# Two gate tiles per weight tile in a wide job, a longer ring in the prologue, and scores inside a values tile

## The reference, cut to what matters

```python
sh_x, sc_x, gt_x = jnp.split((jax.nn.silu(c) @ w_ada[l] + b_ada[l])[:, None, :], 3, axis=-1)
h_x = rms_norm(x, norm_g[l]) * (1 + sc_x) + sh_x
px = split_cols(h_x @ w_in[l])
...
x = x + gt_x * (jnp.concatenate([oa, ob, oc, od], axis=-1) @ w_out[l])
```

## Time and profile before

| what | us |
|---|---|
| median of 3 runs (lowest, highest) | 2264.65 (2260.85, 2273.97) |
| the profiled execution | 2272.0 |
| its span | 2270.2 |
| TensorE matmul busy | 2202.0 (97%) |
| VectorE busy | 1414.0 (62%) |
| ScalarE busy | 1010.9 (45%) |
| GpSimd busy | 99.5 (4%) |
| mean DMA rate | 180 GB/s |

### The profile page before, as it was taken

How to read it: one execution, slowest core, us unless ns; L and a number is a source line. 1 busy time by engine, 2 the same in 40 slices (tenths; PEclk the granted TensorE clock), 3 DMA queues, 4 the chain that set the end, 5 groups by cost and what they waited for, 6 DMA issues and landing times.

```text
span 2270.2 us, 30077 instructions
## 1 busy us (share of the span) xinstructions
PE 2202.0 (97%) x11346; PEld 1817.2 (80%) x11346; DVE 1414.0 (62%) x2097; ACT 1010.9 (45%) x1494; POOL 99.5 (4%) x106
## 2 busy tenths in 40 slices
PE   5999999999999999999989999999999999999998
PEld 1576888997778888888769888888888888888887
DVE  2248654646845676777776544778777877644455
ACT  3343242334545543555466443544444444444453
POOL 1000100102000121000010000000000000000000
PEclk8999999999999999999999999999999999999999
DMA  9976565543035666565501566656665666656674
GB/s 360 357 223 215 195 211 168 159 126 103 11 120 186 197 196 204 159 185 177 185 1 37 171 193 193 207 178 189 183 192 179 187 183 191 200 191 189 191 243 156
DMA packets 209656, 408.18 MB, mean 180 GB/s; under 512 B 15321, under 2 KB 24029, under 8 KB 208076
## 3 DMA queue, kind: packets, MB, share of 16 engines
q1 hardware_dynamic: 205520, 386.71, 54.3%
q0 software_dynamic: 2736, 15.58, 2.3%
q10 hardware_dynamic: 1292, 4.41, 0.5%
HBM read 399.44 MB, written 7.21 MB: 179 GB/s over the span
## 4 chain that ended last, share of the span: by engine, by line
PE 90%; DVE 5%; DMA 3%; ACT 2%; issue 1%; SPq 0%; DVEq 0%; ACTq 0%
PE bank L1984 53%; PE bank L1994 18%; PE bank L1996 9%; DMA ada_ring<-in_w_ada 2%; PE bank L2110 1%; DVE wlo L1221 1%; PE bank L2213 1%; PE bank L2200 1%; PE bank L2127 1%; PE bank L2161 1%; PE bank L2275 1%; PE bank L2362 1%; PE bank L2119 1%; DMA raw<-in_w_in 0%; PE bank L2266 0%
## 5 line engine op out<-in xcount | busy, mean ns | idle before, releaser
L1984 PE MATMUL bank<-whi,xhl 128*128 128x512 f32 (+2 forms) x3776 | 1137.9, 384 | 9.7 <-DVE wlo L1221 8.0
L1221 DVE TENSOR_TENSOR wlo<-raw,whi 128x1024 fp32r<-128x1024 f32 (+2 forms) x649 | 772.5, 1204 | 499.2 <-ACT whi L731 478.2
L731 ACT ACTIVATE whi<-raw 128x1024 fp32r<-128x1024 f32 (+2 forms) x649 | 664.3, 1047 | 673.2 <-PE bank L1984 356.1
L1984 PEld LDWEIGHTS bank<-whi,xhl 128*128 128x128 f32 x3776 | 695.9, 188 | 148.0 <-DVE wlo L1221 10.9
L1984 PE MATMUL bank<-wlo,xhl 128*128 128x512 f32 (+2 forms) x1888 | 720.6, 382 | 0.0
L1994 PE MATMUL bank<-xhl,whi 128*128 128x512 f32 x1792 | 634.4, 399 | 1.4 <-DVE wlo L1221 1.2
L1996 PE MATMUL bank<-xhl,wlo 128*128 128x256 f32 x1792 | 503.3, 281 | 0.0
L1984 PEld LDWEIGHTS bank<-wlo,xhl 128*128 128x128 f32 x1888 | 354.7, 188 | 67.6
L1994 PEld LDWEIGHTS bank<-xhl,whi 128*128 128x128 f32 x1792 | 336.7, 188 | 86.9 <-DVE wlo L1221 3.0
L1996 PEld LDWEIGHTS bank<-xhl,wlo 128*128 128x128 f32 x1792 | 338.5, 189 | 0.0
L1856 DVE TENSOR_TENSOR up_x<-bank,up_x 128x256 f32<-128x256 f32 x88 | 31.2, 417 | 74.2 <-ACT up_x L738 74.2
(11 more groups left out here) (343 smaller groups left out, 1446.6 us busy)
## 6 DMA issues: line engine op xcount, KB each, us to landing
raw<-in_w_in SPq DMA_DIRECT2D x216, 512.0 KB, 4.2
raw<-in_w_up SPq DMA_DIRECT2D x176, 512.0 KB, 3.7
raw<-in_w_out SPq DMA_DIRECT2D x96, 512.0 KB, 4.7
raw<-in_w_down SPq DMA_DIRECT2D x88, 512.0 KB, 4.8
ada_ring<-in_w_ada SPq DMA_DIRECT2D x64, 512.0 KB, 10.1
gate_w<-in_w_ada SPq DMA_DIRECT2D x32, 512.0 KB, 3.8
raw<-in_w_ple_gate SPq DMA_DIRECT2D x32, 512.0 KB, 4.9
raw<-in_w_in SPq DMA_DIRECT2D x16, 384.0 KB, 3.2
```

Source lines behind the costliest of these rows:

```text
L731: nc.scalar.activation(whi[:, slot, 0:size], raw[:, slot, 0:size], ACT.Copy).then_inc(hi_ready, 1)
L1221: tt_(wlo[:, slot, 0:size], raw[:, slot, 0:size], whi[:, slot, 0:size].bitcast(F32), ALU.subtract).then_inc(lo_ready, 1)
L1984: ins = mm(b4[tt][:, 0:width], x[:, o:o + P], w, start=k == 0 and i == 0, stop=k == last and i == 2)
```

## The change

Five things, in the order of the run. The ring of the prologue gets two more slots, of which the eleventh lies over the gain rows, so its first load waits for their transposes; these move from after product 12 to after product 8, the gain loads move from ScalarE's to GpSimd's queue, the bias rows move from the start of GpSimd's stream to after the tables of the heads (and from their own memory into the part of `PX` that job 5 writes), and the in-tiles stand at products 23, 31, 39, and so on. Gate tiles 0 to 7 move from jobs 2 and 3 (every other tile of n = 16 to 30) into job 4, which now has two with each of its eight weight tiles. In the last of the four tiles before unit 8, TensorE makes scores 8 and 9 between the tile's two halves, and VectorE and ScalarE work them before they copy that tile's results out. `Y` is scaled by VectorE in eight pieces, one in each of units 38 to 45. In the second block's scores one mask matmul covers the whole bank.

```diff
-ADA_RING = 9
+ADA_RING = 11
...
-        RPB = at("rpb_rows", 16384, [P, 4, 7, P])
+        RPB = [PX[0:64, h // 2, 2560 + 896 * (h % 2):3456 + 896 * (h % 2)].rearrange("p (r c) -> p r c", r=7)
+               for h in range(4)]
...
-        IN1_TILE = {16 * (k // 2) + (21, 31)[k % 2]: k for k in range(6)}
+        IN1_TILE = {16 * (k // 2) + (23, 31)[k % 2]: k for k in range(6)}
...
-        GATE_AT = {n: g for g, n in enumerate([16, 18, 20, 22, 24, 26, 28, 30]
-                                              + [8 * jj + i for jj in (4, 5, 8) for i in range(8)])}
+        GATE_AT = {**{32 + i: (2 * i, 2 * i + 1) for i in range(8)}, **{40 + i: (16 + i,) for i in range(8)},
+                   **{64 + i: (24 + i,) for i in range(8)}}
...
+                if n == 10:
+                    sp.wait_ge(s_colp, 1)
...
                 load_tile(n, IN1_T[jj][g])
-                if n in GATE_AT:
-                    load_gate(GATE_AT[n])
+                for gate_no in GATE_AT.get(n, ()):
+                    load_gate(gate_no)
...
-                    if X_ROUND[n] == 0:
-                        act.wait_ge(s_rpb, 16)
...
+                if j == J_IN1 + 5:
+                    act.wait_ge(s_rpb, 16)
...
-            phase(N_KV, N_O1, out_kv, later_kv)
-            attend1(8, 32)
+            phase(N_KV, N_O1 - 1, out_kv, later_kv)
+            split(N_O1 + 1)
+            scores1(8)
+            scores1(9)
+            dve.wait_ge(tile_used, N_O1)
+            out_kv(J_KV + 1)
+            attend1(8, 32, True)
...
+                if 38 <= u < 46:
+                    k = u - 38
+                    if k == 0:
+                        dve.wait_ge(rstd, 13)
+                    yv = Y[:, k // 4, (k % 4) * W:(k % 4 + 1) * W]
+                    ts_(yv, yv, ST[:, 120 + k:121 + k], None, ALU.mult).then_inc(y_scaled, 1)
...
-                if n == 12:
+                if n == 8:
                     pe.wait_ge(s_ctx, 10 * 16)
...
+                pe.wait_ge(lo_ready, n + 1)
+                token_major(kv_banks(j), 4, 1, 2 * g, 3, 512, 0, 512, n % RING)
+                scores1(8)
+                scores1(9)
+                token_major(kv_banks(j), 4, 2, 2 * g, 3, 512, 0, 512, n % RING, c0=1).then_inc(tile_used, 1)
```

More of the change, by code:

```diff
@@ L634, in roots_h @@
                 nc.gpsimd.tensor_tensor(s, s, half[:, 0:2], ALU.pow).then_inc(rstd, 1)
[L638 to L642, removed]
+            o = 0
+            for name, k in (("norm_g", 16), ("attn_norm_g_2", 16), ("ffn_norm_g_2", 16), ("ple_norm_g_2", 16),
+                            ("ssm_norm_g_2", 16), ("conv_b_2", 24), ("d_kv_g", 4)):
+                g.dma_start(G1[o:o + k, :], a[name].rearrange("a (k p) -> (a k) p", p=P)).then_inc(s_ctx, 16)
+                o += k
+            g.dma_start(G1[108:124, :], a["b_ada"][0, 2 * D:3 * D].rearrange("(k p) -> k p", p=P)).then_inc(s_ctx, 16)
+            g.dma_start(G2[0:96, :], a["conv_w_2"][0].rearrange("j (k p) -> (j k) p", p=P)).then_inc(s_ctx, 16)
+            g.dma_start(G2[96:128, :], a["b_ada"][0, 0:2 * D].rearrange("(k p) -> k p", p=P)).then_inc(s_ctx, 16)
             g.wait_ge(s_xsq, 1)
@@ L653, in _ @@
             g.dma_start(RTAB[:, :], a["const"][:, K_ROPEH:K_ROPEH + 256]).then_inc(s_tabh, 16)
+            own(nc.gpsimd.memset(PX[0:64, :, 2560:4352], 0.0))
+            for h in range(4):
+                g.dma_start(RPB[h][:, :, 48:79], a["b_rpb"][0, h, 4:11].partition_broadcast(64)).then_inc(s_rpbz, 16)
+            g.wait_ge(s_rpbz, 4 * 16)
+            g.dma_start(rpb_dram.rearrange("p (t c) -> p t c", t=NT), PX[0:64, :, 2560:4352]).then_inc(s_rpb, 16)
             roots(SSQ["A"], 16, P)
@@ L696, in _ @@
             roots(120, 8, 512, group_sums)
[L697 to L701, removed]
             g.wait_ge(pv_done, 32 + 24)
@@ L909, in prob1, with attend1 @@
                 prob(u, S192 if m == "D" else S128, 512, 1, m == "C", PR)
-            def attend1(first, end):
-                prob1(first)
+            def attend1(first, end, begun=False):
+                if not begun:
+                    prob1(first)
                 for u in range(first, end):
@@ L1232, in phase @@
                     split(n)
-                    if n - 1 in GATE_AT:
-                        gate_tile(GATE_AT[n - 1])
+                    for gate_no in GATE_AT.get(n - 1, ()):
+                        gate_tile(gate_no)
                     if n == N_IN1 + 77:
@@ L1469, in key_rope, with attend1 @@
                      RTABD[:, 32 + 64 * t:64 + 64 * t], RT)
-            def attend1(first, end):
-                scores1(first)
-                scores1(first + 1)
+            def attend1(first, end, begun=False):
+                if not begun:
+                    scores1(first)
+                    scores1(first + 1)
                 for u in range(first, end):
@@ L1973, in tile, with token_major @@
                 body().then_inc(tile_used, 1)
-            def token_major(b4, nt, t, k0, last, stride, base, width, slot, xh=XH, xl=XL):
-                for c in range(t):
+            def token_major(b4, nt, t, k0, last, stride, base, width, slot, xh=XH, xl=XL, c0=0):
+                for c in range(c0, t):
                     k = k0 + c
@@ L2373, in _ @@
             pe.wait_ge(o_done, 56)
-            pe.wait_ge(y_scaled, 2)
+            pe.wait_ge(y_scaled, 8)
             jobs(N_O2, J_O2, O2_T, 256, moving=R_O2)
```

25 lines of the change are left out of this document (12 added, 13 removed).

## The result

| | median us | lowest, highest | profiled execution, span |
|---|---|---|---|
| before (4 runs) | 2262.75 | 2260.54, 2273.97 | 2272.0, 2270.2 |
| after (4 runs) | 2298.78 | 2288.52, 2301.46 | 2299.36, 2297.6 |

The change makes the kernel slower, by 1.25%: the ratio is 1.0125, 95% interval 1.0097 to 1.0154. The forecast was 2277 us with a range of 2262 to 2290. The direction was right, the time lies outside.

The account below looks back on a forecast made before the run. TensorE was taken to bound 90% of the chain. Terms -7.4 + 32.7 - 4 - 2.0 - 6.9 sum to +12.4 us, 2284.4 for the profiled execution, given as 2277 us against the median; range 2262 to 2290.

Parts of the forecast that it names:

- the hold: Job 4: two gate slots make each weight load wait for the previous tile's gate pair, 10.6 us per tile; +32.7, bounds 31 to 37.
- I stay at 4.7: Job 4's loop: weight load lands in 4.7 us, the stretch's median; gate-load extremes 3.6 and 6.6 would give 24 and 48.
- Jobs 2 and 3: First projection: without early gate tiles TensorE's 7.8 us standstill goes, save 0.4; -7.4, bounds -7.8 and -4.
- Prologue: Modulation products: bias rows moved, two more ring slots with later in-tiles, and a dry spell; booked -4, bounds -9 and +6.
- (a): Prologue: bias rows leave for the time behind it, saving queue bytes and the slow 10 to 15 us; -4.2, bounds 0 and -4.4.
- (c): Prologue: eleventh slot waits for the gain rows' transposes, so queues run dry about 3.5 us; +3.5, bounds 0 and +8.
- Scores in the values tile: Last values tile: scores made inside it remove most of a 2.6 us TensorE standstill; -2.0, bounds -2.6 and 0.
- Y's scaling: Units near 1180 to 1200 us: moving it from GpSimd to VectorE ends the slowdown, scalings hidden; -6.9, bounds -7 and -3.
- The mask: Second block's scores: one mask matmul per unit leaves the columns the same; 0, bounds -1 and 0.
- Rival B: Job 4: TensorE's clock falls to half in the standstills, wide tiles of 8 us or more; 2283 us, chance 0.12.
- the exit that B had priced: End of job 4: at half clock only tiles 40 and 41 pay, running up to 5.4 us longer; +6 on 2277.
- From execution to median: Whole kernel: the profiled execution before was 7.35 above the median 2264.65, so 2284.4 was given as 2277.

Follow-up runs that it names:

- run 6: Changed kernel with the first gate load of each wide-job pair (tiles 2 to 14, even) cut to 8 of 128 partitions; 2285.01 us, one run.
- run 5: Changed kernel with both gate loads of a pair held until the pair before is used; 2286.2 us, ratio to before 1.0108.
- run 7: Changed kernel with the second gate load of each wide-job pair (tiles 3 to 15, odd) cut to 8 of 128 partitions; 2272.77 us, one run.
- run 2: Kernel before with only the new order of the gate tiles (0 to 15 in pairs in the wide job); 2313.15 us against 2271.7, ratio 1.0177.
- run 3: Changed kernel with six gate slots in place of two for gate tiles 0 to 23; 2250.26 us, ratio to before 0.9887.
- run 4: Changed kernel with four gate slots in place of two; 2245.44 us, ratio to before 0.9888.
- run 9: Kernel before with only the bias rows (memset, four loads, store) moved behind the tables of the heads; 2266.79 us against 2263.61, ratio 0.9997.
- run 10: Six-gate-slot kernel with ten prologue ring slots and no wait for the gain rows' transposes before product tile 10; 2246.43 us, ratio to before 0.9904.
- run 11: Six-gate-slot kernel with one mask matmul per head again in the second block; 2248.97 us, one run.
- run 1: Changed kernel with gate tiles 0 to 7 back in jobs 2 and 3, one per tile in the wide job; 2255.89 us, ratio to before 0.9924.
- run 12: Six-gate-slot kernel with scores 8 and 9 behind the last values tile as before; 2251.05 us, one run.

## Why the forecast was wrong, step by step

**The step that failed is the landing in the hold.** "I stay at 4.7": the loop was written as 8.92 + 1.68 = 10.6 with the landing of the earlier trace rows in it. That landing belongs to a weight load issued 0.41 behind one gate load. The change puts it behind two gate loads that are 1.68 apart, and there it took 6.8. Six loops of 12.7 in place of 10.6 are 12.7 us, and the first landing 2.1 more, 14.8 of the 15.7 by which the hold was under-sized (48.4 against 32.7). The other 0.9 lies in the start: the second gate load of the first held pair went 2.7 us after tile 32's start, and the forecast had 1.8. The mechanism, the place and all other terms of the loop stand: run 6, with the landing put back to 4.7, has the loop of 10.6. Why the landing is 6.8 stays open: the stagger of the two gate loads is part of it (run 5), and neither theory of it held in run 7. The tail of the range was meant for this, but I took the bound from the slowest gate load, 6.6, which gives 48, called it far, and then closed the range at 2290. The 48 came true, by seven landings of 6.4 to 7.0 and the late start, not by eight of 6.6, so that it fits so closely is luck.

**Jobs 2 and 3:** -6.74, with the stage at 44.93 to 44.97 in after and runs 2 to 5; the forecast was -7.4. TensorE stands 0.9 between 185 and 190 us, waiting for VectorE's low part, and the chain ahead of that runs over GpSimd's roots, which take 5.2 (169.04 to 174.22) and leave VectorE idle for 1.67 of it. I had left 0.4 standing.

**Prologue:** -5.24 for -4, a difference that lies within the spread of the copy's start. (a) is -3.6 in run 9 for -4.2. The dip of (c) came where it was forecast, 274 GB/s from 25 to 35 us where before had 377, and is 1.0 MB or 2.7 us of bytes; taking the dip and the eleventh slot out together gained 1.9 in run 10 (at least 1.1), so that slot cost more than it gave. Whether the tenth slot or the later in-tiles bring the rest was not tried.

**Scores in the values tile:** -1.1 for -2.0. The wait that is left came as forecast: the transposes of unit 8 follow the tile at once, and TensorE stands 0.55 us before those of unit 9, where I had put 0.6. What was wrong is the wait before the change. I had read it as 2.6 us, with 0.86 for scores 8 and 9 behind the tile. They are four matmuls that take 1.88, and the row of the transposes behind them gives the standstill as 1.73. From 1.73 to 0.55 is 1.2. Before:

```profile
573.90 1.88 PE L2200 MATMUL bank<-kt,qt 128*128 128x512 f32 x4
577.51 0.66 PE L2127 MATMUL bank<-ident,probs 128*128 128x128 f32 x4 [1.73 <-ACT probs L813]
```

After:

```profile
613.72 0.60 PE L2141 MATMUL bank<-ident,probs 128*128 128x128 f32 x4
...
615.72 0.66 PE L2141 MATMUL bank<-ident,probs 128*128 128x128 f32 x4 [0.55 <-ACT probs L819]
```

**Y's scaling:** -6.9 by run 11, as forecast, within the 1.1 us by which that stage varies. VectorE's eight scalings take 0.48 us each and not 0.32, and stay hidden all the same. **The mask** I had at 0, with -1 as bound, counting columns only; it gave -1.75. For 128-column matmuls that is not enough: one matmul of 512 columns in place of four of 128, each between two others with other weights, saved 0.22 per unit.

**Rival B's mechanism came, and cost nothing in this kernel.** In the standstills, 3.7 to 7.0 us long, TensorE fell to 0.50, and the six wide tiles between 227 and 299 us ran 7.4 to 8.6 us in place of 5.45. Three of them are over 8, which the forecast had named as the sign of B. By the rule of the Trainium skill ("TensorE: Matmul & The Clock Gate", Part 1: The HAM clock gate) an idle array is gated to half its clock; the trace agrees, 0.50 from 225 to 230 us. A loop of 12.7 hides a tile of 8.6, and tile 41, the exit that B had priced, still waited 0.55 us for VectorE. With shorter loops the exit did cost: 1.7 us in run 5 and 1.6 in run 6. Run 3, without standstills, has 1.00 through jobs 4 and 5.

**Two stages that the change doesn't touch:** +1.59 and -1.10. The first is job 9, and it is the clock again, this time without a standstill. In job 9 TensorE makes the gate columns by matmuls of two columns (4.25 us), and behind them it was granted 0.50. That lasted from 433 to 440 us after and cost 3.4 us, from 398 to 402 before and cost 1.7, and did not happen in run 4. Job 9's whole stretch has the same 130 matmuls in all three; the third number from the end is the mean granted clock.

```profile
430.36 4.25 PE L2082 MATMUL bank<-st,gate_acc 128*128 128x2 f32 x32
```

After, before and with four slots:

```profile
425.11:453.69 28.58, 28.58 (x130) 24.12 (x129) 20.66 (x35) 9.78 (x13) 4.19 (x2) 0.88 0.40 112
388.65:415.62 26.97, 26.97 (x130) 22.74 (x129) 20.66 (x35) 9.78 (x13) 4.20 (x2) 0.94 0.43 119
376.24:401.63 25.39, 25.39 (x130) 21.59 (x129) 20.66 (x35) 9.77 (x12) 4.19 (x2) 1.00 0.47 126
```

Which of the three lengths an execution gets doesn't follow the edits: nine other kernels have 27.0 like before, and runs 5 and 11 have 25.4 like run 4. So the 1.6 belongs to none of the theories. The -1.10 is spread as well: that stage is 447.1 to 448.2 us in the 14 kernels, with the same code there.

**What cancels.** The whole sum is 15.0 too small. The hold alone is 15.7; the other terms and the untouched stages come to -0.7 only because they go both ways (+0.7 jobs 2 and 3, -1.2 prologue, +0.9 scores, -1.8 units with the mask, +0.7 untouched).

**From execution to median:** I took 7.35 off, the distance of before's profiled execution from its median. After's own distance was 0.6. That is 6.8 us of the total miss of 21.8; the other 15.0 is in the table. Both profiled executions had the longer feed-forward part. By their times most of before's other executions had the shorter one, which would explain the 7.35, but no profile of them shows it.

Four kernels beat the one before with an interval clear of 1: runs 1, 3, 4 and 10 (runs 11 and 12, variants of run 3, have one execution each). Six slots with the ring of ten has a profiled run of 2247.29 with the longer feed-forward part, against 2272.0 for before with the same, 1.1% less; the interval of its ratio is 0.9871 to 0.9938. The intervals of runs 3, 4 and 10 overlap, so none of them is shown to be the best.

## What to carry to other kernels

When an in-order queue issues both the critical loads and a side stream with its own few slots, count over how many tiles the wait of the side stream reaches back; going from two tiles to one turned a hidden loop of 8.9 us per two tiles into an open one of 12.7 per tile. Two more slots took all but 0.2 us of the loss away, where cutting one of three loads to a sixteenth took only 13 to 16 us of 48. Take a landing time only from a load in the same company, with as many others ahead of it and as far apart as after the change; if the trace has none, the bound, not the median of near rows, decides the range. Compare by landmarks rather than by totals: a part that no edit touches moved the totals by 9 us, more than five of the six terms of the sum. Landmarks vary too, by 1.6 us in the old prologue and by 3.2 in job 9, and the granted clock of the stage should be looked at before a difference of that size is explained by an edit.

## What the runs showed of the hardware

- Three 512 KB loads in one queue land 8.9 us after the first issue when issued at 0, 1.68 and 2.10 (after), and 6.6 when issued at 0, 0.5 and 0.9 (run 5). The queues show a hole of 107 GB/s in the first case. With a small load in the middle the third lands at 6.5 (run 7). In a queue kept full the same stagger (run 3, 203 to 225 us) has no microsecond under 227 GB/s. Here the hole is only seen where the queue had run empty before. Why is open.
- TensorE fell to the lower of its two levels (1.2 GHz, granted 0.50) at 225 us in a standstill that had begun at 220.3, and was back at 1.00 from 232 us on, in the tile that began at 227.3.
- It fell to the same level without a standstill, behind 4.25 us of matmuls with two columns: for 6.8 us in after, 3.4 in before, and not at all in run 4.
- Per-head mask matmuls of 128 columns between others cost 0.07 us each more than their columns (0.22 for three, run 11); at 256 columns nothing.
- The 1792 feed-forward matmuls with 512 columns take 399 ns in nine profiled executions and 393 in five, 8.6 to 9.9 us in all, whatever the edit.
